# Newton steps of the reciprocal square roots on GpSimd instead of VectorE, in a two-layer decoder step on eight cores

## What is computed

```python
def rmsnorm(x, g):
    y = x * rsqrt(mean(x * x, -1) + EPS)
    return y * g
# layer 0: x += 0.5*SwiGLU(rms(x)); x += GLA(rms(x)); x += 0.5*SwiGLU(rms(x))
# shared K/V: k, v = proj(rms(x)); k = rope(rmsnorm per head(k))
# layer 1: x += 0.5*SwiGLU(rms(x)); q = rope(rmsnorm per head(proj(rms(x))))
#          x += dilated window attention(q, k, v) @ w_out; x += 0.5*SwiGLU(rms(x))
# GLA: its output is normed per head too: rmsnorm(o, out_norm) * silu(r)
```

## Time and profile before

| | |
|---|---|
| median of 3 runs | 2458.86 us (2457.78 to 2463.61) |
| profiled execution: time, span | 2456.32 us, 2454.8 us |
| spans of the 8 cores | 2444.3 to 2454.8 us |
| mean granted TensorE clock, by core | 0.992 to 0.994 of full speed |
| TensorE busy | 2339.2 us, 95% |
| VectorE busy | 1387.4 us, 57%, 3520 instructions |
| ScalarE busy | 621.4 us, 25% |
| GpSimd busy | 228.2 us, 9%, 431 instructions |

### The profile page before, as it was taken

The page is one execution under the profiler, slowest core; times in us unless marked ns, Lnnn a source line. Parts: engine busy times, 40 slices in busy tenths (PEclk is TensorE's granted clock), DMA queues, the critical chain, the costliest instruction groups (busy, mean ns, idle before and its releaser), DMA issues.

```text
span 2454.8 us, 45772 instructions; the slowest of 8 cores (2444.3 to 2454.8 us)
## 1 busy us (share of the span) xinstructions
PE 2339.2 (95%) x16455; PEld 1183.8 (48%) x16754; DVE 1387.4 (57%) x3520; ACT 621.4 (25%) x1124; POOL 228.2 (9%) x431
## 2 busy tenths in 40 slices
PE   3998999999979999999999999999999999999999
PEld 1444445545535555445444544444454454444444
DVE  4433565656556556567346634586766757674333
ACT  2102234133244324123012301133231331311010
POOL 0000000100100010000100100001111001000000
PEclk9999999999989999999999999999999999999999
DMA  5447454665635555644544553435865436345444
GB/s 121 70 73 147 77 89 95 123 101 82 108 60 88 88 100 95 111 81 100 103 68 79 117 84 65 76 66 81 149 105 96 76 60 112 59 90 114 68 77 114
DMA packets 85950, 225.10 MB, mean 92 GB/s; under 512 B 10672, under 2 KB 24800, under 8 KB 85600
## 3 DMA queue, kind: packets, MB, share of 16 engines
q0 software_dynamic: 63152, 191.70, 47.9%
q1 hardware_dynamic: 22576, 30.47, 3.9%
HBM read 398.40 MB, written 15.40 MB: 169 GB/s over the span
## 4 chain that ended last, share of the span: by engine, by line
PE 83%; DVE 7%; issue 7%; DMA 2%; ACT 1%; DVEq 0%; SPq 0%; ACTq 0%
PE ps L444 77%; PE ps L453 6%; DMA xT<-xp 2%; DVE sm L471 1%; DVE mix L471 1%; DVE mix L468 1%; DVE sm L468 1%; ACT mix L461 1%; DVE sm L478 0%; DVEq L307 0%; SPq L484 0%; DVE act L468 0%; DVE hT L471 0%; DVE th L471 0%; ACT L461 0%
## 5 line engine op out<-in xcount | busy, mean ns | idle before, releaser
L444 PE MATMUL ps<-hT,wF 128*128 128x512 bf16 (+1 forms) x6543 | 1229.3, 339 | 24.5 <-DVE sm L478 7.7
L444 PEld LDWEIGHTS ps<-hT,wF 128*128 128x128 bf16 x6720 | 550.3, 98 | 618.1 <-issue 29.0
L444 PE MATMUL ps<-act,wF 128*128 128x512 bf16 (+1 forms) x3277 | 607.4, 337 | 9.0 <-DVE act L468 4.2
L461 ACT ACTIVATE th<-ps 128x512 f32<-128x512 f32 (+1 forms) x420 | 210.1, 516 | 970.2 <-PE ps L444 894.8
L471 DVE SCALAR_TENSOR_TENSOR th<-th,ps 128x512 f32<-128x512 f32 (+1 forms) x420 | 240.0, 585 | 363.5 <-ACT th L461 362.8
L444 PEld LDWEIGHTS ps<-act,wF 128*128 128x128 bf16 x3360 | 274.4, 97 | 304.4 <-issue 6.4
L471 DVE SCALAR_TENSOR_TENSOR xT<-ps,xT 128x512 f32<-128x512 f32 x256 | 176.0, 688 | 260.5 <-PE ps L444 254.7
L444 PE MATMUL ps<-mix,wM 128*128 128x512 bf16 (+2 forms) x1532 | 292.1, 339 | 9.0 <-DVE sm L471 5.1
L468 DVE TENSOR_TENSOR act<-th,ps 128x512 bf16<-128x512 f32 (+1 forms) x420 | 244.9, 586 | 92.7 <-PE ps L444 81.8
L444 PEld LDWEIGHTS ps<-mix,wM 128*128 128x128 bf16 (+1 forms) x1560 | 128.6, 97 | 149.0 <-issue 13.8
L484 POOL DMA_DIRECT2D wF<-wfi x168 | 88.8, 529 | 983.8 <-PE ps L444 836.2
(11 more groups left out here) (72 smaller groups left out, 1119.3 us busy)
## 6 DMA issues: line engine op xcount, KB each, us to landing
wF<-wfi POOLq DMA_DIRECT2D x168, 512.0 KB, 6.0
wF<-wfo POOLq DMA_DIRECT2D x64, 352.0 KB, 4.6
wF<-wfo POOLq DMA_DIRECT2D x64, 320.0 KB, 4.4
xT<-xp SPq DMA_DIRECT2D x8, 1024.0 KB, 16.0
wM<-wgqk POOLq DMA_DIRECT2D x16, 512.0 KB, 5.4
wM<-wgv POOLq DMA_DIRECT2D x16, 512.0 KB, 5.2
wM<-wgr POOLq DMA_DIRECT2D x16, 512.0 KB, 5.2
wM<-wgo POOLq DMA_DIRECT2D x16, 512.0 KB, 5.8
```

The source lines that it names most:

```text
L444: ins = e.matmul(R(out), lhsT=l, rhs=r, start=(start and i == 0), stop=(i == len(pairs) - 1))
L461: S.op(ACT, lambda e: e.activation(out=out, in_=R(in_), func=func, scale=scale, bias=bias), reads, writes, dur=0.19 + fsz(out) * 0.834e-3)
```

## The change

In rsqrt_small the nine instructions of the three Newton steps and the two of the split into hi and lo leave VectorE and run on GpSimd, through a new helper g that records an operation on GpSimd with an assumed duration of 0.12 us. The instruction a = -0.5 * a * m, and y = (a + 1.5) * y, became three: a = a * m, a = -0.5 * a + 1.5, y = y * a. So a Newton step has four instructions instead of three, and a call has 3 steps on VectorE and 14 on GpSimd.

```diff
         v_ts(m, ps_in, scale, EPS, MUL, ADD, [K("ps", bkey)], [k])
+
+        def g(fn):
+            S.op(PL, fn, [], [k], dur=0.12)
         v_ts(i0.bitcast(I32), m.bitcast(I32), 1, None, ALU.logical_shift_right, None, [], [k])
         v_ts(y.bitcast(I32), i0.bitcast(I32), -1.0, float(MAGIC), MUL, ADD, [], [k])
         for _ in range(3):
-            v_tt(a, y, y, MUL, [], [k])
-            v_stt(a, a, -0.5, m, MUL, MUL, [], [k])
-            v_stt(y, a, 1.5, y, ADD, MUL, [], [k])
-        v_copy(hi, y, [], [k])
-        v_tt(lo, y, hi, SUB, [], [k])
+            g(lambda e: e.tensor_tensor(out=a, in0=y, in1=y, op=MUL))
+            g(lambda e: e.tensor_tensor(out=a, in0=a, in1=m, op=MUL))
+            g(lambda e: e.tensor_scalar(out=a, in0=a, scalar1=-0.5, scalar2=1.5, op0=MUL, op1=ADD))
+            g(lambda e: e.tensor_tensor(out=y, in0=y, in1=a, op=MUL))
+        g(lambda e: e.tensor_copy(out=hi, in_=y))
+        g(lambda e: e.tensor_tensor(out=lo, in0=y, in1=hi, op=SUB))
         return hi, lo, k
```

## The result

The changed kernel takes **2516.6 us** (median of 4 runs, 2514.5 to 2522.2), the kernel before, on the same chip, 2458.3: a ratio of **1.0239**, interval 1.0223 to 1.0255. The forecast was 2512 us, with slower at 0.83.

A forecast was written before the change was run, and what follows sets the result against it. TensorE was taken as the bound, with chain latency deciding. Waits at the spread +59 us and VectorE's relief -6 gave +53, from 2456.3 to 2509 us profiled, predicted as 2512 with the median's 2.6 offset; range 2460 to 2655.

The forecast's parts named there:

- The bound and the mechanism: Whole kernel: TensorE, busy 95% of the span, waits at spreads in fixed order; chain latency decides, not busy time.
- What leaves VectorE: In rsqrt_small calls: 1045 instructions or 155 us leave VectorE, giving back half of 12.8 us of waits, -6 us.
- s = 0.38: GpSimd chains: 0.38 us from one step's start to the next, so 14 steps take 5.3 us.
- 0.6 us for an issue inside: GpSimd's queue: each of 51 weight-load issues inside chains costs 0.53 us plus a gap, 0.6 us.
- What cover the new order leaves: TensorE's work between sum and spread leaves 4.2 us for 14 steps in A, 4.6 us in B.
- the sum: All spreads: 80 us of waits in place of 20.8, +59; less 6 for VectorE, +53 us.
- A: The 55 calls of 1 or 4 columns (norms, GLA heads): 55 x (5.3 - 4.2) = 61 us of waits.
- B: The 40 calls of 2 or 8 columns (rotary norms in K/V, attention): 28 us, a third off for shared stalls: 19.
- (1): GpSimd steps as quick as VectorE's, about 0.27 us: most waits go, 2428 to 2450 us, faster; chance 0.08.
- (2): Heavy GpSimd steps of 0.5 to 0.64 us: +191 to +354 us, 2650 to 2813 us; chance 0.16.
- (3): Attention stages: VectorE's 32 two-SBUF-input additions hold up GpSimd steps, +22 us, 2534; no chance of its own, within 0.67.
- (4): GpSimd's queue: chains wait behind issues whose slot frees late, +40 us, 2552; no chance of its own, within 0.67.

The follow-up runs named there:

- e4: The changed kernel in its own order, with the third Newton step's four GpSimd instructions left out of each call; 1.0022 of the kernel before.
- e1: The changed kernel with the planner told 0.23 us for a GpSimd step instead of 0.12, order planned anew; 1.0042 of the kernel before.
- e7: The changed kernel with the planner told 0.04 us for a GpSimd step instead of 0.12, same instructions; 1.0711 of the kernel before.
- e3: The changed kernel, order kept, with weight-load issues inside a chain on GpSimd moved behind its last step; 1.0156 of the kernel before.

## Why the prediction was right, and where it was off

**The bound and the mechanism: right.** TensorE's order and the latency of the chain decide: e4, e1 and e7 move the waits to 31, 21 and 166 us with after's arithmetic or less of it.

**"What leaves VectorE": right, and worth nothing.** 1045 instructions left, and busy time on sm fell from 197.1 to 45.4:

```profile
0.00:2512.70 2512.70, 45.43 (x285) 0.99 0.51 90
```

The page's total fell by 125 us, not by the forecast 155: part of the small steps overlaps its neighbours in the records (in the earlier trace rows the 0.68 us tile starts before the 0.16 us step ends). The -6 us on the 12.8 of sm waits did not come. Away from the start the rows of sm steps went from 10.4 to 5.3 us, but the 5.13 are the wait that changed its name; the two others, 4.56 and 0.71 us, are as long in after. At the start the row grew (3.12 to 7.10). VectorE's relief gave TensorE nothing back.

**"s = 0.38": 0.34.** It lies between the forecast and the low end, 0.27; the high end, 0.64, was far off. GpSimd by line (mean ns of one, then idle time and its releasers) answers to the earlier trace rows:

```profile
L545 POOL TENSOR_TENSOR sm<-sm 128x4 f32<-128x4 f32 (+3 forms) x285 | 58.4, 207 | 29.2 <-POOL sm L544 0.4 <-POOL smb L549 0.3
...
L544 POOL TENSOR_TENSOR sm<-sm 128x4 f32<-128x4 f32 (+3 forms) x285 | 56.9, 202 | 169.4 <-DVE sm L478 140.2 <-DVE mix L471 5.6 <-PE ps L444 2.9
L546 POOL TENSOR_SCALAR sm<-sm 128x4 f32<-128x4 f32 (+3 forms) x285 | 55.2, 196 | 33.1 <-POOL sm L545 32.1 <-DVE sm L478 0.2
```

**"0.6 us for an issue inside": 0.79.** The gap before it is 0.30, not VectorE's 0.11. The two issues of the first chain, one step apart, cost 1.16 us together, as the text had it (1.2). The first spread came at 27.98 where the text had some 29, since the sum ended 0.5 us earlier (20.99) and 14 steps were 0.04 shorter each.

**"What cover the new order leaves", and the sum: the total nearly right, its parts not.** The forecast had 61 us of waits in A and 19 in B. Measured are 22.5 in A (28 places), 30.2 in B (28), 17.5 in the start and 5.3 of others; before has 7.0, 6.6, 11.2 and 10.4. In A, the formula at s = 0.34 gives 55 x (4.76 - 4.2) = 31. In B it gives 40 x 0.16 x 2/3 = 4, against 30: **this is the step that failed**, and it failed in the chain and not in the cover.

TensorE's work between sum and spread is 7.29 us on average in the 40 calls of B, where the text had 7.3. But the last step ends 8.4 us after the sum and the spread can start 0.15 later, 8.5 in all, where the text's terms with s = 0.34 come to 7.4. Most of the difference is one term: the text gave 0.22 us to two handovers (the earlier trace rows show 0.12 and 0.15), none to the new one from VectorE to GpSimd, and let GpSimd begin as soon as VectorE's third step was done. In 30 of the 40 calls it began more than 0.2 us after that, 33 us later in all than the 0.15 that a free GpSimd takes, because it was still in the steps of another chain or in an issue. One of them, in VectorE and GpSimd (the third step ends at 1834.26, and the first Newton step, L544 at 1836.68, stands behind the other chain's):

```profile
1834.09 0.17 DVE L478 TENSOR_SCALAR sm<-sm 128x8 int32<-128x8 int32 x1
...
1835.43 0.20 POOL L547 TENSOR_TENSOR sm<-sm 128x8 f32<-128x8 f32 x1
...
1835.92 0.60 POOL L484 DMA_DIRECT2D wF<-wfi  x1 [0.29 <-POOL sm L547]
1836.53 0.20 POOL L548 CAST smb<-sm 128x8 bf16<-128x8 f32 x1
1836.68 0.20 POOL L544 TENSOR_TENSOR sm<-sm 128x8 f32<-128x8 f32 x1
```

The text knew that another chain's steps stand between in 30 of the 40, and took it only as a reason to take a third off. The mean hides something too, but less: with 7.4 us for each call and each call's own work in between (4.6 to 9.9 us) the shortfalls add up to 19 us, where the mean gives 6; with the chains as long as they were they add up to 51. With the third taken off that is 12 and 34, against the 30 measured.

**Luck in the total.** With the measured s the text's own sum is 31 + 4 = 35 us of waits, 14 above the 20.8, less 6: +8 us or 2467 us. The s that was too high stood in for the late starts of the chains. The sum took +59 of waits where +45 came, -6 for VectorE where nothing came, and nothing for the clock, which took 11.5 us; these errors cancel to +53 against +58 on the slowest core. The direction and the mechanism don't rest on that.

**The rivals.** (1) and (2) fall with s = 0.34. (3), the two engines holding each other up, exists but is small: of 1330 GpSimd steps 21 are over 300 ns, 8.4 us more than usual in all, against the 22 us priced. Each of the 21 lies beside an addition of VectorE with both inputs in SBUF (`mix<-mix`), 15 of them beside the 32 additions of the earlier trace rows. These are as long as they were (691 ns on average), and the longest step is about as long as one of them; length and count of after's steps (duration ns min/median/max):

```profile
L545 POOL TENSOR_TENSOR sm<-sm x285: 179/199/762, 22.3 to 2272.6; 128x4 f32<-128x4 f32 x64, 128x8 f32<-128x8 f32 x48, 32x1 f32<-32x1 f32 x19, 32x2 f32<-32x2 f32 x12
```

The Trainium skill ("SBUF — State Buffer", "SBUF: two separate sides") has the rule that a VectorE instruction with two SBUF inputs and a GpSimd instruction that reads SBUF exclude each other for a whole instruction; the trace agrees with it in these 21 steps, and here it decides nothing. (4), a queue that an issue blocks, is small: nine issues with a chain waiting behind them waited longer than the usual 0.30 us, by 0.3 to 1.2 us each and 5 us in all, against the 40 priced, and e3, which moves the issues inside chains away, leaves 63 of the 75 us of waits. GpSimd's queue did hold chains up, but with the steps of other chains and with issues ahead of a chain's first step, which no rival had.

## What to carry to other kernels

When a chain of tiny dependent instructions moves to an idle engine, count its latency from start to start against the work that the order puts in front of its consumer, call by call, and start it where the engine's queue really lets it start: behind the other chains and issues that stand there. The relief of an engine that bounds nothing is worth nothing. Where a planner sets the order, the length that it is told is part of the change: the same instructions took 1.0042, 1.0239 and 1.0711 of before with 0.23, 0.12 and 0.04 us in the plan. Keep exposed places, such as the start, on the quickest engine, and expect that added idle time of TensorE can cost more than itself, through the clock: here 11.5 us on the slowest core and nothing on core 6.

## What the runs showed of the hardware

- A GpSimd step on 1 to 8 columns is busy for 0.20 us and starts 0.34 us after the one it depends on; VectorE's take 0.16 and 0.27. The size does not matter, nor does the number of inputs: in the first call of after, 24.89 to 25.93, L545 (two inputs) to L546 is 0.36, L546 (one input) to L547 0.34, L547 (two) to L544 0.34.
- The Trainium skill's read cost ("GPSIMD Engine Reference", Performance pitfalls for Q7 kernels), from which the prediction estimated 0.29 us with one input and 0.38 with two, would show a difference of 0.09 between those rows. It is not there; only the mean of the two estimates agrees.
- A DMA issue on GpSimd inside a chain of dependent steps costs 0.79 us: 0.30 of idle time before it, 0.60 of its own, and the normal gap saved. A second issue one step behind the first adds 0.39.
- GpSimd steps that catch a VectorE addition of two SBUF tiles can last up to 0.76 us in place of 0.20: 21 of 1330 here.
- Many small waits went with a lower clock. In e7 74 places wait for smb, the granted clock of the slowest core is 0.970, where before has 0.992, and the same 16754 matmuls are busy for 2408.1 us, 2372.3 in after and 2360.8 on core 3 of before. This is an observation over the runs, since none changes the clock alone, and cores with the same waits differ in it (0.987 and 0.994 in after).
